# Two convolution feed-forwards take the unscaled residual row, and VectorE sums and scales both halves at once

## The reference, cut to what matters

```python
def conv_ffn(x, w_up, conv_w, conv_b, w_down):
    u = x @ w_up
    s = u.shape[1]
    half = CONV_W // 2
    up = jnp.pad(u, ((0, 0), (half, half), (0, 0)))
    c = conv_b
    for j in range(CONV_W):
        c = c + conv_w[j] * up[:, j:j + s]
    g, val = c[..., :FFN_HIDDEN], c[..., FFN_HIDDEN:]
    return (jax.nn.gelu(g) * val) @ w_down
...
        h = h + rms_norm(a, norm_g[i, 1])
        f = conv_ffn(rms_norm(h, norm_g[i, 2]), ffn_w_up[i], ffn_conv_w[i], ffn_conv_b[i], ffn_w_down[i])
        h = h + rms_norm(f, norm_g[i, 3])
```

## Time and profile before

| | us |
|---|---|
| runs, median of 3 | 1144.75 (1144.3 to 1144.89) |
| the profiled execution, its own time | 1143.86 |
| its span | 1142.1 |
| TensorE busy | 1123.6 |
| VectorE busy | 818.7 |
| ScalarE busy | 696.9 |

### The profile page before, as it was taken

How to read it: one execution, slowest core, us unless ns; L and a number is a source line. 1 busy time by engine, 2 the same in 40 slices (tenths; PEclk the granted TensorE clock), 3 DMA queues, 4 the chain that set the end, 5 groups by cost and what they waited for, 6 DMA issues and landing times.

```text
span 1142.1 us, 19048 instructions
## 1 busy us (share of the span) xinstructions
PE 1123.6 (98%) x6594; PEld 972.7 (85%) x6594; DVE 818.7 (72%) x1263; ACT 696.9 (61%) x1227; POOL 48.6 (4%) x71
## 2 busy tenths in 40 slices
PE   9999999999999999999999999999999899999997
PEld 7987888888899878888888888888997788888886
DVE  5866888888756578888887766666656746766665
ACT  6656666766566666766666554546585836555553
POOL 0100000000100010000000000000000320000000
PEclk9999999999999999999999999999999989999999
DMA  8705666756344455666654766655683006875761
GB/s 261 243 1 161 183 201 196 217 178 217 121 138 144 159 155 171 211 195 200 200 170 146 221 200 185 196 172 140 203 263 146 1 11 174 223 218 171 204 159 64
DMA packets 237172, 194.74 MB, mean 171 GB/s; under 512 B 11230, under 2 KB 219712, under 8 KB 237120
## 3 DMA queue, kind: packets, MB, share of 16 engines
q1 hardware_dynamic: 237040, 194.01, 56.5%
q10 hardware_dynamic: 80, 0.03, 0.0%
HBM read 192.97 MB, written 1.05 MB: 170 GB/s over the span
## 4 chain that ended last, share of the span: by engine, by line
PE 92%; DVE 4%; ACT 2%; issue 1%; POOL 1%; DMA 0%; POOLq 0%; DVEq 0%; ACTq 0%
PE psum L918 26%; PE psum L923 14%; PE psum L951 7%; PE psum L954 7%; PE psum L958 7%; PE psum L696 6%; PE psum L698 6%; PE psum L697 6%; ACT arena L2049 1%; PE psum L752 1%; DVE resid_eps L2242 1%; PE psum L904 1%; PE psum L1203 1%; PE psum L908 1%; PE psum L905 1%
## 5 line engine op out<-in xcount | busy, mean ns | idle before, releaser
L918 PE MATMUL psum<-act_hl,hi_u 128*128 128x512 f32 x1312 | 326.9, 391 | 0.0
L2152 DVE TENSOR_TENSOR lo_u<-raw_u,hi_u 128x2048 fp32r<-128x2048 f32 x103 | 236.0, 2292 | 93.7 <-ACT hi_u L1575 54.6
L918 PEld LDWEIGHTS psum<-act_hl,hi_u 128*128 128x128 f32 x1312 | 240.6, 188 | 46.4
L923 PEld LDWEIGHTS psum<-act_hl,lo_u 128*128 128x128 f32 x1312 | 179.0, 190 | 12.8
L923 PE MATMUL psum<-act_hl,lo_u 128*128 128x256 f32 x1312 | 182.9, 282 | 0.0
L1593 ACT ACTIVATE hi_u<-raw_u 128x2048 fp32r<-128x2048 f32 x68 | 129.7, 1907 | 12.4 <-DMA raw_u<-in_ffn_w_gu 12.3
L1712 ACT ACTIVATE arena<-psum 128x256 f32<-128x256 f32 x174 | 64.7, 376 | 101.7 <-PE psum L923 94.0
L2307 DVE TENSOR_TENSOR arena<-psum,arena 128x256 f32<-128x256 f32 x174 | 72.9, 421 | 72.4 <-ACT arena L1712 72.2
L2157 DVE TENSOR_TENSOR lo_d<-raw_d,hi_d 128x1024 fp32r<-128x1024 f32 x88 | 106.8, 1217 | 8.5 <-ACT hi_d L1602 8.5
L2335 DVE SCALAR_TENSOR_TENSOR arena<-arena,vecs 128x255 f32<-128x255 f32 x176 | 84.9, 482 | 37.9 <-ACT arena L1720 26.9
L2124 DVE TENSOR_TENSOR lo_u<-raw_u,hi_u 128x1024 fp32r<-128x1024 f32 (+6 forms) x84 | 78.1, 970 | 27.5 <-ACT hi_u L1572 27.3
(11 more groups left out here) (311 smaller groups left out, 1796.3 us busy)
## 6 DMA issues: line engine op xcount, KB each, us to landing
raw_u<-in_ffn_w_up SPq DMA_DIRECT2D x88, 512.0 KB, 5.6
raw_d<-in_ffn_w_down SPq DMA_DIRECT2D x86, 512.0 KB, 3.4
raw_u<-in_ffn_w_gu SPq DMA_DIRECT2D x84, 512.0 KB, 5.7
raw_u<-in_diff_w_qkv SPq DMA_DIRECT2D x24, 512.0 KB, 4.6
raw_u<-in_w_in SPq DMA_DIRECT2D x24, 512.0 KB, 4.4
raw_u<-in_mla_w_o SPq DMA_DIRECT2D x8, 512.0 KB, 4.4
raw_u<-in_diff_w_o SPq DMA_DIRECT2D x8, 512.0 KB, 4.3
raw_u<-in_w_out SPq DMA_DIRECT2D x8, 512.0 KB, 4.4
```

The costliest lines, as they stand in the source:

```text
L918: pe.matmul(o, hi[:, k, :], act_hl[:, k].rearrange("p a t -> p (a t)"), start=k == 0, stop=False)
L923: mm = pe.matmul(o[:, SEQ:], lo[:, k, :], act_hl[:, k, 0, :], start=False, stop=k == KC - 1)
L2152: dve.tensor_tensor(v[0], v[1], v[2].bitcast(F32), ALU.subtract).then_inc(S("lo_u_done"), 1)
```

## The change

N_F0 and N_F1, the norms ahead of the two convolution feed-forwards, join `UNSCALED`. Their row isn't scaled into `normed`; TensorE transposes the residual row. The factors are transposed in up(1) as in f=2 and f=3. In the body VectorE waits for both cross copies, adds gate and value in one operation of 512 columns (`both_summed`), and multiplies both by `row_factors` in a second one of 512 (`both_scaled`). The raw sums go into `cross`, the scaled ones into `up_sum`. ScalarE makes both cross copies first, then both middle taps, then gelu and the rest; in tile 0 the high weights of tile 2 come ahead of the middle taps. In tile 0 VectorE makes the low weights of tile 2, copies the factors, and then multiplies.

```diff
-UNSCALED = [N_F2, N_F3]
+UNSCALED = [N_F0, N_F1, N_F2, N_F3]
...
-WARM_UNSCALED = {N_DIFF: (2, 5), N_F2: (2, 5), N_F3: (0, 0)}
+WARM_UNSCALED = {N_F0: (2, 5), N_F1: (2, 5), N_DIFF: (2, 5), N_F2: (2, 5), N_F3: (0, 0)}
...
-                        if isinstance(t, int) and t == 1 and s == 0 and f >= 2:
+                        if isinstance(t, int) and t == 1 and s == 0 and i in UNSCALED:
                             factors_turn(i)
...
-            norm_transposes(N_F0)
+            resid_transposes(N_F0)
...
                     if b is None and t < 2:
                         if 1 not in crossed:
                             cross_out(1)
-                        if f < 2:
+                        if t == 1 and f < 2:
                             conv_mid(0, cg)
+                            conv_mid(1, cv)
                         split_u(u + 2)
+                        if t == 0 and f < 2:
+                            conv_mid(0, cg)
+                            conv_mid(1, cv)
                     elif f < 2:
+                        cross_out(1)
                         conv_mid(0, cg)
-                        cross_out(1)
+                        conv_mid(1, cv)
                     if f < 2:
                         act.wait_ge(S("tap_b"), at2(2 * g + 1))
                         act.activation(gg[0:n, slot, :], cg[0:n, slot, :], ACT.Gelu_apprx_tanh).then_inc(S("gated"), 1)
-                        conv_mid(1, cv)
...
+                    def both_summed():
+
+                        dve.wait_ge(S("cross_out"), at2(2 * g + 2))
+                        dve.tensor_tensor(cross[:, slot], psum[:, 4 + 2 * slot:6 + 2 * slot, 0:SEQ], cross[:, slot], ALU.add)\
+                            .then_inc(S("gate_raw"), 1)
+
+                    def both_scaled():
+
+                        dve.wait_ge(S("gate_raw"), at(g + 1))
+                        dve.tensor_tensor(up_sum[:, slot], cross[:, slot], row_factors.unsqueeze(1).broadcast_to([P, 2, SEQ]),
+                                          ALU.mult).then_inc(S("up_sum"), 2)
...
-                    sum_up(0)
-                    if f >= 2 and (b is not None or t):
-                        gate_scaled()
+                    if f < 2:
+                        both_summed()
+                        if b is not None or t:
+                            both_scaled()
+                    else:
+                        sum_up(0)
+                        if b is not None or t:
+                            gate_scaled()
...
+                    if b is None and t == 0:
+                        split_u(u + 2)
+                        factors_out()
+                        if f < 2:
+                            both_scaled()
+                        else:
+                            gate_scaled()
                     if f < 2:
                         taps(0, cg)
-                    if b is None and t < 2:
+                    if b is None and t == 1:
                         split_u(u + 2)
...
-            norm(N_F0)
+            resid_norm(N_F0)
```

More of the change, by code:

```diff
@@ L1692, in resid_norm @@
                     high(i, k)
-                    if i == N_F3 and k in (3, 7):
+                    if i in (N_F0, N_F1, N_F3) and k in (3, 7):
                         split_part(SECOND[i], k // 4)
@@ L2100, in _ @@
             diff()
-            norm(N_F1)
+            resid_norm(N_F1)
             ffn(1)
@@ L2320, in factors_out @@
                     def factors_out():
-                        i = N_F2 if f == 2 else N_F3
+                        i = [N_F0, N_F1, N_F2, N_F3][f]
                         s = st[:, ST_OF[f"norm{i}"]]
                         dve.wait_ge(S("factors_tr"), UNSCALED.index(i) + 1)
-                        ch.put(dve.tensor_scalar(s[:, 8:10], s[:, 0:2], FACTOR[i + 1], None, ALU.mult))
+                        if f >= 2:
+                            ch.put(dve.tensor_scalar(s[:, 8:10], s[:, 0:2], FACTOR[i + 1], None, ALU.mult))
                         ch.link(dve.tensor_copy(row_factors, psum[:, 0, 0:SEQ]))
@@ L2351, in tile @@
                         hidden_low(g - 1, 1 - slot, P)
-                    if b is None and t < 2:
+                    if b is None and t < 2 and f >= 2:
                         sum_up(1)
@@ L2355, in tile @@
                         hidden_low(g - 1, 1 - slot, P)
+                    if b is None and t == 0:
[5 more added lines that the diff above has]
+                            gate_scaled()
                     if f < 2:
                         taps(0, cg)
-                    if b is None and t < 2:
+                    if b is None and t == 1:
                         split_u(u + 2)
-                        if f >= 2 and t == 0:
-                            factors_out()
-                            gate_scaled()
-                    elif n == P:
+                    elif n == P and f >= 2 and (b is not None or t):
                         sum_up(1)
```

6 lines of the change are left out of this document (3 added, 3 removed).

## The result

| us | before | after |
|---|---|---|
| runs | 1144.82 (1144.3 to 1145.7) | 1158.39 (1157.5 to 1162.44) |
| profiled execution: span | 1142.1 | 1155.7 |
| TensorE / VectorE / ScalarE busy | 1123.6 / 818.7 / 696.9 | 1124.9 / 841.5 / 688.8 |
| mean granted clock of TensorE | 0.994 | 0.992 |

The change is slower: ratio 1.0125 (95% interval 1.0111 to 1.0138).

The account below looks back on a forecast made before the run. The prediction took TensorE, busy 98% of the span, as the bound. For each feed-forward -2.54 (head) + 4.27 (first tiles) + 3.8 (last tile) + 1.7 (clock) = +7.23 us, so 1159.2; own range 1157 to 1162, 8 in 10 1150 to 1168.

Parts of the forecast that it names:

- Bound: Whole kernel: TensorE holds 98% of the span, so a change costs wherever it makes TensorE's queue wait.
- Head: Last residual row to the end of the first "up": 2.54 us less in each convolution feed-forward.
- VectorE's turn: Body, one tile of VectorE's loop: grows from 7.74 to 8.11 us, staying 0.20 under TensorE's 8.31.
- Rival (b): Body: VectorE's turn is longer than TensorE's tile; +5 us for each feed-forward, 1169; chance 12%.
- First tiles: From P0 (end of the first "up") to tile 4's low products: a serial chain makes TensorE 4.27 us late.
- Last tile: From P21 (start of the last full "down") to the last "down": late hidden tile leaves TensorE idle 3.8 us.
- Clock: Behind each last tile's wait: TensorE's granted clock drops, costing 1.7 us, with bounds 0 and 3.4.
- Rival (a): Behind the last tile's wait: the clock stays up, so 1155.8; chance 20%.
- Sum: Both convolution feed-forwards: +7.23 us each, +14.5 in all, giving 1159.2 on the runs' scale.
- The sign: Whole kernel: slower than before, chance 0.88; faster 0.07, no measurable change 0.05.
- range of 8 in 10: Whole kernel: the measured time lies between 1150 and 1168 us with a chance of 8 in 10.
- Rival (d): Whole kernel: the heads' gain lands and the first and last tiles' stalls stay away, 1139.7; chance 7%.

Follow-up runs that it names:

- g_halves: The kernel before with the unscaled head in both convolution feed-forwards, but four VectorE passes of 256 where the change has two of 512; 1178.09 us, ratio 1.0293.
- c_table: The changed kernel with a ScalarE gelu on two columns ahead of tile 0's constants, so the activation table loads in a wait; 1158.69 us.
- f_first: The changed kernel with another order of VectorE's and ScalarE's work in the first tiles, including the early table load; 1155.12 us, ratio 1.0088.
- h_tail: The changed kernel with VectorE's low weights for the next stage's first unit moved from tile 20 into its waits in tile 21; 1160.29 us.
- b_warm: The changed kernel with 12 TensorE matmuls on zeros in the wait for the last hidden tile of both convolution feed-forwards; 1157.85 us.
- a_copy: The changed kernel as it is, measured and profiled again in a second series; 1162.12 us, ratio 1.0156.
- m_before: The kernel before with TensorE matmuls on zeros, 6 each, aimed at two mixer waits, one set standing one level too late; 1143.81 us, ratio 0.9994.
- e_pool: The changed kernel with the multiplication of both halves by the row's factors on GpSimd, in both convolution feed-forwards; 1214.58 us, ratio 1.0623.

## Why the prediction came out as it did

- **Bound.** Right. Waits of TensorE where it had none, and its clock behind the last of them, are the whole loss, and VectorE's longer busy time (22.8 us more) is itself not in the sum.
- **Head.** Right to 0.01 us; f=2 was an exact model of it.
- **VectorE's turn.** 8.14 for 8.11. Rival (b) stayed away, by 0.17 us a tile; g_halves shows what it would have been. The 0.03 x 16 are 0.5 of lag more at tile 20.
- **First tiles.** Right in sum (4.33 for 4.27) and mostly in its parts: the first hidden tile, 118.58 + 0.43 in the trace, 10.35 behind P0 for 10.41, tile 1's 18.38 (126.62 + 0.42) for 18.41, tile 4's low weights 28.32 (134.69 + 2.29) for 28.31. The wait of 0.81 at tile 4 is for its high weights; the other waits are 0.16 to 0.75. The prediction counted the table load in full, and in the trace it does stand in the row in full, 7.14 to 8.42 behind P0 for 7.19 to 8.47. c_table shows that hiding it gives back only 0.7, since gelu then waits for VectorE's first taps, and f_first that another order as a whole gives back 2.5.
- **Last tile.** The size was near (4.14 and 4.28 for 3.8, most of it two waits of 0.66 and 3.05), the step behind it only half right. Tile 20's sum starts 1.48 us behind the end of its "up" (275.27 - 273.79), for 0.7 + 0.4 predicted, and this lag is where the difference comes from: the last sum starts 2.61 behind P21 for 2.2, and the chain behind it takes 5.54 (to 290.25) for 5.7. I put VectorE's 9.38 us of tile 20 down as work in a row (measured 9.44). h_tail took 1.22 us of that work away and the distance stayed. What ends last is ScalarE's high "down" weights, behind its high weights for the next stage, and then VectorE's low ones ahead of the sum. I had read VectorE's queue and not the wait in it, which the trace of before has too (timeline of VectorE, tile 20 of f=0); the 9.38 stood near the measured value although 0.55 of it was a wait.

```profile
276.68 2.36 DVE L2157 TENSOR_TENSOR lo_d<-raw_d,hi_d 128x1024 fp32r<-128x1024 f32 x2 [0.49 <-ACT hi_d L1602]
```

- **Clock.** 1.66 in f=0 for 1.7; 2.58 in f=1, between the forecast and the bound of 3.4. Rival (a), that it stays up, did not come. The term belongs to its place, as b_warm shows. What the prediction missed is that the mixer, which the change doesn't touch, moves by 5 us from one execution of the same kernel to the next (after -2.9 against before, a_copy +2.0).
- **Sum.** The two feed-forwards cost 16.4 us, not 14.5, and in the profiled execution the mixer gave 2.9 back. The agreement of 1159.2 with 1158.39 therefore owes something to chance: the second series has 1162.12. The sign and the range of 8 in 10 hold for both; the forecast's own 1157 to 1162 holds for the first and just misses the second. Of the mechanism, head, first tiles and clock hold, and the last tile's in part, as said above.
- **Rival (d), faster**, is shut for the orders tried: with the better orders and the clock kept up, about 3.5 us a feed-forward are still missing. That a wholly other last tile could do it (its gate half first, as in before) is open: g_halves had it, but with VectorE as the bound, which hides what it could bring.

## What to carry to other kernels

Work that is taken out of an engine's way once (a head, 2.5 us) and put back in small pieces into another's loop pays at the loop's ends, where there is no slack, before it pays in the middle: cost the first and the last tile as chains across engines, and ask of each instruction in them what it waits for, not only how long the queue is. Compare distances between the same instructions of two traces, and span times mean clock (good to about 0.6 us with a clock of three decimals), before a difference of a few us between times is believed. Fill a wait with matmuls on zeros only where TensorE really waits; in m_before, one level beside it, they brought nothing.

## What the runs showed of the hardware

**GpSimd and VectorE slow each other.** In e_pool the same 512-wide multiply takes 1.28 us while VectorE waits, and 2.13 beside VectorE's low weights (two timelines, first tiles):

```profile
113.84 1.28 POOL L659 TENSOR_TENSOR arena<-arena 128x512 f32<-128x512 f32 x1 [4.75 <-DVE arena L2355]
120.22 1.29 POOL L659 TENSOR_TENSOR arena<-arena 128x512 f32<-128x512 f32 x1 [5.10 <-DVE arena L2330]
130.69 2.13 POOL L659 TENSOR_TENSOR arena<-arena 128x512 f32<-128x512 f32 x1 [9.17 <-DVE arena L2330]
```
```profile
120.91 1.69 DVE L2170 TENSOR_TENSOR lo_d<-raw_d,hi_d 128x1024 fp32r<-128x1024 f32 x1 [0.83 <-ACT hi_d L1611]
```

Where GpSimd came first (120.22), VectorE's low "down" weights took 1.69 us for the usual 1.22. The Trainium skill, "GPSIMD Engine Reference", section 8, says that GpSimd shares its SBUF interfaces with VectorE and contends with VectorE's instructions that have two SBUF inputs; the low weights are such, and the rows agree. GpSimd's operation at 206.42 (2.14 us, shown above) began while 0.99 us of VectorE's were left and took 0.86 longer than alone, nearly as if it had waited them out. My expectation had taken GpSimd's 1.05 to 1.3 us from the mixer.

**The clock behind equal waits differs.** The wait ahead of L1472 (1.67 us in before, 1.66 in a_copy and after) was followed by 8 us at 0.57 in before and a_copy, and by 1.00 in after. What decides between them stays open.
